# Rows loaded a second time in turned form, norm taken on the projected rows, and a sample stage ordered around query weights in four column blocks

## What is computed

```python
def rms_norm(x, g):
    y = xf * lax.rsqrt(jnp.mean(xf * xf, axis=-1, keepdims=True) + EPS)
    return (y * g.astype(jnp.float32)).astype(x.dtype)

z = rms_norm(h, norm1_g) @ w_in            # 1024 -> 2304: queries, keys, values of groups A and B
oa = attn_a(...)                           # 8 heads, band of 9 chunks of 64 rows, learned bias
ob = attn_b(...)                           # 8 heads on 2 key heads, band of 3 chunks, sinks
h = h + concat(rms_norm(oa, ga), rms_norm(ob, gb)) @ w_out
...
q = (xb @ w_query).reshape(PEER_BLOCK, PEER_HEADS, 2, D_HALF)      # xb = rms_norm(h, norm2_g)
s = jnp.einsum('thpd,hpkd->thpk', q, sub_keys)
sv, si = lax.top_k(s, PEER_TOPK)           # 16 of 128 for each of 16 half heads
cand = sv[:, :, 0, :, None] + sv[:, :, 1, None, :]
fv, fi = lax.top_k(cand, PEER_TOPK)        # 16 of the sums for each of 8 heads
eidx = jnp.take_along_axis(cidx, fi, axis=-1)
a = jnp.einsum('thkd,td->thk', expert_u[eidx], xb)
w = jax.nn.softmax(fv) * jax.nn.gelu(a, approximate=False)
out = jnp.einsum('thk,thkd->td', w, expert_v[eidx])
```

## Time and profile before

| | |
|---|---|
| Median of 3 runs | 3794.66 us (3793.25 to 3795.22) |
| Profiled execution | 3796.45 us, of it 3794.6 us span |
| Before tile 0's queries and keys are turned (weights in, tile 0 projected) | 0 to 50.9 us |
| Tiles 0 to 7 | 50.9 to 621.95 us |
| Sample stage, up to the first gather | 621.95 to 798.48 us |
| Experts | 798.48 to 3794.6 us |
| PE busy, DVE busy, ACT busy | 2750.9, 2313.9, 698.1 us |
| Gather queue | 1217 MB, 78.1% of 16 DMA engines' span |

### The profile page before, as it was taken

One profiled execution on the slowest core, in us unless ns is written; L12 is line 12 of the kernel. 1 busy time (PEld: TensorE's weight loads), 2 busy tenths in 40 slices (PEclk: granted clock), 3 DMA queues, 4 the chain that ended last, 5 costly groups with the idle time before them and its releaser, 6 DMA issues.

```text
span 3794.6 us, 39042 instructions
## 1 busy us (share of the span) xinstructions
PE 2750.9 (72%) x13359; PEld 1028.7 (27%) x13359; DVE 2313.9 (61%) x6166; ACT 698.1 (18%) x2341; POOL 1091.4 (29%) x1179
## 2 busy tenths in 40 slices
PE   7999997767766766776667667666766766776665
PEld 4455544732212211221222122122212212221111
DVE  2333342747766775776677577667757766875544
ACT  2333332211112111111211111111111111111111
POOL 0000000023333333333333333333333333333332
PEclk9999998767867777776787788678778767776666
DMA  5000003259999999999999999999999999999998
GB/s 200 17 17 17 23 30 146 83 223 406 421 421 405 404 421 401 421 399 422 402 421 403 406 421 407 421 403 421 403 407 421 403 422 406 408 413 421 421 421 335
DMA packets 193446, 1277.37 MB, mean 337 GB/s; under 512 B 22624, under 2 KB 26336, under 8 KB 44384
## 3 DMA queue, kind: packets, MB, share of 16 engines
q0 software_dynamic: 167184, 1217.47, 78.1%
q1 hardware_dynamic: 26064, 57.42, 4.2%
HBM read 1255.40 MB, written 12.32 MB: 334 GB/s over the span
## 4 chain that ended last, share of the span: by engine, by line
PE 37%; DMA 35%; DVE 11%; issue 7%; ACT 6%; POOL 3%; SPq 1%; DVEq 0%; POOLq 0%; ACTq 0%
DMA arena<-in_experts,arena 34%; PE PS L1319 14%; PE PS L1136 7%; DVE arena L921 6%; PE PS L1346 5%; POOL arena L593 3%; ACT arena L801 3%; PE PS L1229 3%; PE PS L1305 2%; PE PS L1113 2%; PE PS L1218 1%; PE PS L1178 1%; ACT arena L795 1%; DVE arena L1000 1%; DVE arena L997 1%
## 5 line engine op out<-in xcount | busy, mean ns | idle before, releaser
L921 DVE CUSTOM_DVE_ANT_0 arena<-arena,PS 128x1024 f32<-128x1024 f32 x1152 | 1382.4, 1219 | 932.8 <-DMA arena<-in_experts,arena 486.7
L593 POOL DMA_INDIRECT arena<-in_experts,arena x1152 | 1082.8, 940 | 2031.4 <-PE PS L1319 1622.6
L1305 PE MATMUL PS<-arena 96*128 96x512 bf16 x2304 | 827.8, 460 | 825.4 <-DVE arena L921 778.5
L1319 PE MATMUL PS<-arena 128*32 128x512 f32 x4608 | 931.3, 952 | 111.2 <-ACT arena L801 60.2
L1305 PEld LDWEIGHTS PS<-arena 96*128 96x128 bf16 x2304 | 162.9, 104 | 1532.0 <-DVE arena L921 1278.9
L795 ACT ACTIVATE arena<-arena 128x4 f32<-128x4 f32 x288 | 59.2, 205 | 2047.3 <-DVE arena L921 2035.8
L1319 PEld LDWEIGHTS PS<-arena 128*32 128x32 f32 x4608 | 164.3, 150 | 683.9 <-issue 380.6
L1346 PEld LDWEIGHTS PS<-arena 128*128 128x128 f32 x2304 | 277.0, 200 | 86.4 <-issue 86.2
L1136 PE MATMUL PS<-arena 128*128 128x512 f32 (+1 forms) x720 | 287.6, 552 | 3.8 <-ACT arena L627 2.3
L1346 PE MATMUL PS<-arena 128*128 128x128 f32 x2304 | 290.0, 287 | 0.0
L801 ACT ACTIVATE arena<-arena 128x1 f32<-128x1 f32 x1152 | 244.8, 283 | 9.9 <-ACT arena L795 0.2
(11 more groups left out here) (129 smaller groups left out, 1579.3 us busy)
## 6 DMA issues: line engine op xcount, KB each, us to landing
arena<-in_experts,arena POOLq DMA_INDIRECT x1152
arena<-in_w_in SPq DMA_DIRECT2D x4, 2048.0 KB, 15.7
arena<-in_w_query POOLq DMA_DIRECT2D x8, 1024.0 KB, 16.9
arena<-arena SPq DMA_DIRECT2D x108, 64.0 KB
h_scratch<-arena SPq DMA_DIRECT2D x9, 512.0 KB, 2.6
arena<-h_scratch SPq DMA_DIRECT2D x9, 512.0 KB, 8.2
out<-arena SPq DMA_DIRECT2D x9, 512.0 KB
arena<-in_x_prompt SPq DMA_DIRECT2D x8, 512.0 KB, 3.5
```

Source lines behind the costliest of these rows:

```text
L593: pool.indirect_dma_start(out=uv[r], out_offset=None, in_=experts, in_offset=bass.IndirectOffsetOnAxis(ap=expert_T[t % 2][:, tok:tok + 1], ...
L921: dve.tensor_tensor_reduce(uv[r][:, 0:D], uv[r][:, 0:D], xb(n), 1.0, 0.0, ALU.mult, ALU.add, a_dot[(n // 4) % 2][:, n % 4:n % 4 + 1]).then ...
L1305: mm = pe.matmul(PS[:, 2 + 2 * (n % 2) + c, :], pick[0:96, j:j + 1].broadcast_to([96, P]), x3[t % 2][0:96, g, 512 * c:512 * c + 512], star ...
L1319: mm = pe.matmul(PS[32 * g:32 * g + 32, ACC + c, :], wz[n % 2][:, g, 31 - f:63 - f], uv[r][:, D + 512 * c:D + 512 * c + 512], start=(f == ...
```

## The change

Four things are changed.

1. **Turned rows are loaded.** The host also passes `xT`, the rows of each tile already turned. SP loads a tile of it (`load_turned`), POOL multiplies it by the gain (`gain`, one elementwise instruction of 128x1024). The eight transposes on PE, their two copies on DVE and the scaling of the rows on DVE are gone; ACT now applies 1/rms when it copies a projected block out. `w_in` comes in ten loads of half a block each.
2. **The projection is dealt out by single products.** `FILL` gives, for each step, how many products stand ahead of `weigh` and `turn` and how many behind. While tile 7 runs, `FILL_SAMPLE` puts all 40 products of the sample tile into steps 0 to 4.
3. **The sample stage is reordered.** The query weights come through SP in four blocks of 512 columns, each with a semaphore of its own, among the other loads. The norm of tile 0's rows moves ahead of tile 7's residuals, the turned `x2T` between its output products, the first query product ahead of stream 0. ACT scales the streams' probabilities (DVE keeps the reciprocals). `stream_values(b)` stands one iteration later on PE. The steps of the selection are dealt out anew, 48 of 160 units in the last iteration.
4. **The end of the stage.** The experts' numbers are turned and copied before the gates, and the residuals follow.

```diff
-PIECES = range(7)
-PIECE_AT = {m: m for m in PIECES}
+PIECES = range(5)
+FILL = ((2, 4), (2, 4), (4, 2), (2, 4), (2, 2), (2, 2), (2, 2), (2, 2))
+FILL_SAMPLE = ((2, 6), (2, 6), (2, 6), (2, 6), (2, 6), (0, 0), (0, 0), (0, 0))
-FIRST_SHARE = (0, 29, 29, 29, 29, 15, 15, 15)
+FIRST_SHARE = (20, 26, 26, 10, 10, 10, 10, 48)
+FIRST_LEAD = (0, 6, 6, 6, 6, 6, 6, 0)
...
+                def load_turned(t):
+                    if t:
+                        sp.wait_ge(proj_psum, 5 * t)
+                    sp.dma_start(xT.rearrange("p a b -> p (a b)"), xT_in[t * P:(t + 1) * P, :]).then_inc(xT_loaded, 16)
...
+                load_turned(1)
                 sp.dma_start(x_sb[1], x_prompt[P:2 * P, :]).then_inc(x_in[1], 16)
...
                         if t + 2 < NT:
                             rows = x_prompt[(t + 2) * P:(t + 3) * P, :] if t + 2 < NT_PROMPT else x_sample
                             sp.dma_start(x_sb[(t + 2) % 3], rows).then_inc(x_in[(t + 2) % 3], 16)
+                    if t + 2 < NT:
+                        load_turned(t + 2)
...
                 store_kv(NT_PROMPT)
+                sp.wait_ge(proj_psum, 5 * NT)
+                sp.dma_start(g2_bc, g2[0:1, :].broadcast_to([P, D])).then_inc(g2_in, 16)
+                load_query_weights(0)
+                sp.dma_start(subk_sb.rearrange("p a b -> p (a b)"), subk).then_inc(subk_in, 16)
                 sp.wait_ge(s_read, 16 * NT_PROMPT)
                 sp.dma_start(bias_s_sb, bias_s).then_inc(bias_s_in, 16)
                 load_keys(0)
+                load_cached_values(0)
+                load_query_weights(1)
...
+                load_query_weights(2)
+                load_query_weights(3)
                 store_h(NT_PROMPT - 1)
                 spread(0)
...
+                def gain(t):
+                    if t == 0:
+                        pool.wait_ge(g1_in, 16)
+                    pool.wait_ge(xT_loaded, 16 * (t + 1))
+                    pool.tensor_tensor(xT, xT, g1_sb.unsqueeze(2).broadcast_to([P, KD, P]), ALU.mult).then_inc(xT_ready, 1)
+
+                gain(0)
...
                 pool.memset(bias_a_sb[64:P, :, 0:64], NEG).then_inc(masks, 1)
                 pool.wait_ge(masks, 4)
-                pool.wait_ge(proj_psum, 5 * NT)
-                for k in range(KD):
-                    pool.dma_start(w_query_sb[:, k, :], w_query[k * P:(k + 1) * P, :]).then_inc(w_query_ready, 16)
+                for t in range(1, NT):
+                    gain(t)
...
-                        act.copy(v_ring[t % V_RING], PS[:, UNIT, :]).then_inc(z_ready, 1)
+                        act.activation(v_ring[t % V_RING], PS[:, UNIT, :], ACT.Copy, scale=scale).then_inc(z_ready, 1)
...
+                def stream_normalise(b):
+                    q = b % 2
+                    act.wait_ge(drcp_ready, b + 1)
+                    for r in range(2):
+                        for g, cols in enumerate((S_A, S_B)):
+                            w, c = sc_s[2 * q + r][:, cols], 4 * q + 2 * g + r
+                            act.activation(w, w, ACT.Copy, scale=rcp[:, c:c + 1]).then_inc(dp_ready, 1)
...
                 route(0, "shift")
+                out_rms(NT_PROMPT)
+                route(0, "turned")
                 route(0, "gates")
-                out_rms(NT_PROMPT)
-                residual(NT_PROMPT, 0)
-                residual(NT_PROMPT, 1)
-                route(0, "turned")
-                residual(NT_PROMPT, 2)
-                residual(NT_PROMPT, 3)
+                for i in range(4):
+                    residual(NT_PROMPT, i)
...
+                for l in range(4):
+                    route(0, "q", 0, l)
                 for b in range(STREAMS):
                     if b + 1 < STREAMS:
                         stream_scores(b + 1)
+                    if b:
+                        stream_values(b - 1)
                     stream_turn(b)
-                    if b == 0:
-                        route(0, "x2T")
-                    if 1 <= b <= 4:
-                        route(0, "keys", b - 1)
-                    stream_values(b)
                     if b < 4:
+                        route(0, "keys", b)
+                    if b < 3:
                         for l in range(4):
-                            route(0, "q", b, l)
+                            route(0, "q", b + 1, l)
+                stream_values(STREAMS - 1)
```

248 lines of the change are left out of this document (131 added, 117 removed).

## The result

The changed kernel takes 3745.82 us in the median of 4 runs (3741.54 to 3746.68), the kernel before 3794.94 us beside it (3793.25 to 3798.31). The ratio is 0.9867, with an interval from 0.9851 to 0.9882: it is faster by 1.3%. The profiled execution took 3746.12 us, 3744.3 of it span; the prediction had 3739.9 for it, and 3738 for the median.

A forecast was written before the change was run, and what follows sets the result against it. PE is busy 92 to 96% in tiles 1 to 6; in the sample stage only chains count. `turned` moves from 797.6 to 597 + 144 = 741 us, -56.6, the experts' part unchanged: median 3738, range 3718 to 3762.

The forecast's parts named there:

- Step 1: Tile 0: projections end 6 us earlier, but bias tables queue behind them; `reduce` 5 us later, tile 0 +6 us.
- Step 2: Tiles 1 to 7: transposes removed, PE waits filled with products, slow stretches gone; 30.9 us saved.
- Step 3: Sample stage: query weights travel earlier, selection starts at T + 34 instead of T + 66.7.
- T: Moment when the turning of tile 8 starts; forecast at 597 instead of 621.95 us.
- Step 4: Sample stage: late key loads make rounds of 12.5 us; selection ends at T + 140, 15 us longer than now.
- Rival B: Key loads not late, DVE alone sets sample stage; selection ends near T + 125; 3714 to 3728 us, chance 0.22.
- Step 5: After the selection: output products done by T + 143, norm sums bind `turned`, which ends at T + 144.
- The sign I gave for it: Tail: `turned` comes within 5 us of the last `experts` step.
- C: Tiles give half, products ahead of `turn` delay it: 31 becomes 16 us; 3748 to 3762 us, chance 0.22.
- D: Tiles wait for POOL's slow gain, kernel slower than before: above 3802 us, chance 0.03.
- the cover of 14 us: Tiles: 14 us of slack beyond load 3.6 and gain 2.3 before tile t+2's turned rows are needed.
- E: Query weights no sooner; selection starts 25 to 32 us later than T + 34; 3763 to 3770 us, chance 0.05.

The follow-up runs named there:

- Experiment 1: Changed kernel with the load of tile 1's turned rows moved behind the bias tables in SP's queue; 3735.75 us, ratio 0.9829.
- Experiment 4: Changed kernel with the projection of tiles 1 to 7 back in whole blocks of eight products at a step's end; 3775.8 us in one execution.
- experiment 3: Changed kernel with bias tables before tile 1's turned rows, keys before values, and stream 2's keys ahead of tile 7's h store; 3715.63 us, ratio 0.9777.
- experiment 2: Changed kernel with SP's sample-stage loads reordered, keys b+1 ahead of values b; 3731.25 us, ratio 0.9819.
- experiment 9: Changed kernel with PE's turning of the experts' numbers ahead of the sample tile's output products; 3751.88 us, ratio 0.9878.
- experiment 7: Changed kernel with nine more POOL passes over the turned rows ahead of each gain for tiles 1 to 8; 3810.88 us, ratio 1.0034.
- experiment 5: Changed kernel with tile 8's projection dealt over all eight steps of tile 7 instead of steps 0 to 4; 3755.71 us, ratio 0.9885.
- Experiment 12: Kernel of experiment 3 with the norm of the next tile's rows one four later on ACT and DVE; 3716.68 us, ratio 0.9782.

## Why the prediction was right, point by point

The size was right to 8 us of 57, and the mechanisms mostly. The span's error is 6.3 us (3744.3 against 3738.0): 3.1 at the constants, 4.0 in the tiles, 2.6 in the tail, less 3.5 that the experts' part gave back. Those 3.5 us are luck: that part was carried over unchanged, no run explains them, and four executions of the changed kernel differ by 5 us. Without them the median would have missed by 11.

**Step 1, the opening.** Right in mechanism. Projections of tile 0 ended at 45.6 for 44.9: PE started at 7.99, held by weights and not by the gain, and ACT's copy with the scale takes 0.69 us where the plain one takes 0.58. `bias_b` landed at 62.9 for 59.7; the term mis-sized is the transfer, 17.3 us from the first issue to this landing where I had 12.8 + 2. I had taken 410 GB/s throughout, but in the slices of 1.75 us from 45.5 and from 50.75 the engines moved only 56 and 107 GB/s. `reduce` was 8.3 us late for 5, outside my 2.5 to 6.5, and tile 0 ended 9.1 late for 6. Experiment 1 shows the mechanism. I named the wait and gave it 5 us; I did not say that it hides a possible gain of 11.

**Step 2, the tiles.** Tiles 4 to 6 were forecast at 18.5 us and gave 17.5; no wait was left in steps 0 and 1. Tiles 1 to 3 gave 7.1 for 8.4, tile 7 2.3 for 4, with its clock down at the end. I had split off 1.0 us for transposes in each tile. Experiment 4 says that this split doesn't hold, though the sum did: by themselves the missing transposes are worth nothing where PE waits anyway.

**Step 3, the selection's start.** T + 34.15 for T + 34. The h store was issued at T + 21 and landed 9.8 us later, at T + 31 for T + 28. What I missed is that keys 2 stand behind it: scores 2 waited 4.6 us, and experiment 3 puts it at 5.2, by difference.

**Step 4, the selection.** The three late key loads came as told, in rounds of 13.0 us for 12.5, and the selection ended at T + 138.1 for T + 140, since the last part was shorter: from the end of scores 7 it took 25 us for 28.4. I had read 58 units off the table of shares; steps are not split, and as they are dealt 49 stand behind stream 7, 4 us less. Rival B, that the loads are not late, was false here, and experiment 2 built it: 16.1 us for the 15 that I had between the two.

**Step 5, the tail.** The step that failed. I had PE done with both output products at T + 143 and `turned` bound by the norm sums. PE has them at T + 146: stream 7's scores at 715.16, two rounds of values with waits for ACT and squares of 3.58, at the lower clock, and products of 9.93, with a granted clock of 0.71. The sign I gave for it fell too: `turned` came 8.5 us behind the last `experts` step, not within 5. From the selection's end the tail took 8.5 us for the 4 I had. The selection was 1.9 us early, so `turned` came only 2.6 late against T, which is luck too. And behind it stood an assumption that I did not price, that `turned` carries over one for one. It does while the whole chain moves (experiments 1 to 3: 11.0, 16.1 and 32.3 us of it are 9.2, 14.7 and 32.3 us of span in the profiled executions), and it doesn't when only the numbers move ahead of the residuals (experiment 9).

**The other rivals.** C did not occur: the waits of PE in tiles 1 to 6 come to one of 0.3 us. D was far off, with 1.90 us for the gain; experiment 7 made it true, at ten times the gain, and found the cover of 14 us that the prediction had worked out, but each wait dearer than I had it. E did not occur, and experiment 5 shows a mild form.

**The page.** POOL's gain took 1.90 us, where the 4497 ns for 2048 elements in the Trainium skill, "GPSIMD Engine Reference", section "Elementwise — side-by-side cycle accounting", made 2.2 an estimate; the measurement decides. By the rule in its section "Engine selection" the work belongs on DVE, which would have had it sooner. In tile 0's opening that was worth nothing, as PE was released by a load 0.7 us behind the gain's end. But I had written that the gain runs beside everything but the opening, and that is wrong. A DVE instruction that started during the gain ended with it: 1.84 us for 0.16 in experiment 1, and 1.31 for 0.17 (L916, from 64.82) in the changed kernel, where the gain for tile 1 runs from 64.21 to 66.11. No wait of PE over 0.3 us in tiles 1 to 6 comes of it. The gain on DVE was not run.

## What to carry to other kernels

When a load with a wait is put into a queue, read every load written behind it: here three such places held 32 us more, beside a change that gave 49. A wait of 3 to 4 us on a dense matrix engine is dearer than it is long, so single products placed in it pay more than whole blocks at a step's end. And a moment such as `turned` is only worth what the ring behind it can use: look at the refills, not at the first issue. Experiment 12 shows that the first refill alone doesn't tell it either: it came 4.9 us sooner and the time stayed.
